# A 14-stage transformer kernel in split float32: the square sums of each stage's entry before the last step of k, weight units asked for one at a time over the first feed-forward pairs, and the keys' scaled input in a place of its own

## The reference

```python
# first block: retention layer ("ret"), then latent attention ("lat")
h = retention_layer(x, ...)                      # q, k, v, gate projections; 8 heads; group norm; w_out_a
k_nope, k_rope, v = shared_latent_kv(h, ...)     # w_kv_a, rmsnorm of the latent, w_uk, w_uv
h = mla_layer(h, ...)                            # w_in_b, w_uq, softmax attention, gate, w_out_b
# second block: short convolution ("mix") in layer 0, differential attention ("dif") in layer 1
for i in range(2):
    h = rms_norm(x, g_pre_mix[i])
    mix = short_conv_mixer(h, ...) if i == 0 else diff_attention(h, k, v, ...)
    # where i == 1: k, v = split(rms_norm(x, g_kv) @ w_kv), a gain of its own on the same x
    x = x + rms_norm(mix, g_post_mix[i])
    # "ffn0", "ffn1"
    gate, up = split(causal_dwconv(rms_norm(x, g_pre_ffn[i]) @ w_up), 2)
    x = x + rms_norm((silu(gate) * up) @ w_down, g_post_ffn[i])
    # "ple0", "ple1"
    g = sigmoid(rms_norm(x, g_pre_ple[i]) @ w_gate)
    x = x + rms_norm(g * (p[i] @ w_proj), g_post_ple[i])
```

## Time and profile before

| | |
|---|---|
| median of 3 runs | 2166.62 us |
| the profiled execution | 2169.12 us |
| its span | 2167.3 us |
| PE busy | 1997.5 us (92%) |
| DVE busy | 1220.8 us (56%) |
| ACT busy | 824.7 us (38%) |
| granted TensorE clock, mean | 0.965 of full speed |

### The profile page before, as it was taken

The page is one execution under the profiler, slowest core; times in us unless marked ns, Lnnn a source line. Parts: engine busy times, 40 slices in busy tenths (PEclk is TensorE's granted clock), DMA queues, the critical chain, the costliest instruction groups (busy, mean ns, idle before and its releaser), DMA issues.

```text
span 2167.3 us, 25399 instructions
## 1 busy us (share of the span) xinstructions
PE 1997.5 (92%) x9756; PEld 1666.3 (77%) x9756; DVE 1220.8 (56%) x1981; ACT 824.7 (38%) x1339; POOL 379.6 (18%) x300
## 2 busy tenths in 40 slices
PE   7999999988889999988999999798998889999996
PEld 6888888867678777876888787677787768887875
DVE  6565665256555454356777524566664577774245
ACT  4232323233465433333444323335454344442232
POOL 3322331111232210120111011221011211110111
PEclk9999999989999999999999999899999999999998
DMA  4222222222111233322223322231111212333311
GB/s 162 82 74 93 78 83 88 88 67 81 60 38 49 71 101 103 103 73 78 97 98 98 107 87 78 68 114 55 58 40 59 82 65 97 97 108 107 97 64 54
DMA packets 53664, 178.91 MB, mean 83 GB/s; under 512 B 6151, under 2 KB 8711, under 8 KB 53544
## 3 DMA queue, kind: packets, MB, share of 16 engines
q1 hardware_dynamic: 53544, 177.29, 24.7%
HBM read 172.55 MB, written 4.72 MB: 82 GB/s over the span
## 4 chain that ended last, share of the span: by engine, by line
PE 55%; DVE 12%; ACT 5%; issue 4%; POOL 1%; DVEq 0%; POOLq 0%; ACTq 0%
PE pb L780 51%; DVE WL L763 3%; ACT WH L754 2%; DVE X L947 1%; DVE FR L981 1%; PE pb L880 1%; ACT T L967 1%; PE pb L864 1%; PE pb L2405 0%; PE pb L1993 0%; DVE T L941 0%; DVE FD L1979 0%; PE pb L868 0%; DVE FD L1982 0%; ACT T L2543 0%
## 5 line engine op out<-in xcount | busy, mean ns | idle before, releaser
L780 PE MATMUL pb<-FR,WH 128*128 128x512 f32 x4552 | 1443.8, 399 | 93.3 <-DVE WL L763 40.8
L780 PEld LDWEIGHTS pb<-FR,WH 128*128 128x128 f32 x4552 | 861.3, 192 | 291.5 <-issue 57.2
L780 PE MATMUL pb<-FR,WL 128*128 128x512 f32 x2276 | 899.8, 395 | 0.0
L763 DVE TENSOR_TENSOR WL<-stage,WH 128x1024 fp32r<-128x1024 f32 x311 | 409.1, 1336 | 502.1 <-ACT WH L754 501.5
L780 PEld LDWEIGHTS pb<-FR,WL 128*128 128x128 f32 x2276 | 435.5, 191 | 93.8
L754 ACT ACTIVATE WH<-stage 128x1024 fp32r<-128x1024 f32 x311 | 318.2, 1051 | 116.9 <-PE pb L780 104.1
L780 PE MATMUL pb<-WH,FR 128*128 128x256 f32 x832 | 155.8, 285 | 3.8 <-DVE T L1098 1.5
L780 PE MATMUL pb<-FR 128*128 128x256 f32 (+3 forms) x752 | 124.3, 316 | 21.3 <-DVE T L1305 12.2
L780 PEld LDWEIGHTS pb<-FR 128*128 128x128 f32 x752 | 112.7, 195 | 36.0 <-DVE T L1305 14.8
L780 PEld LDWEIGHTS pb<-WH,FR 128*128 128x128 f32 x832 | 131.6, 192 | 5.1 <-DVE T L1098 1.9
L973 POOL TENSOR_TENSOR acc<-acc,T 128x512 f32<-128x512 f32 x56 | 75.3, 1344 | 276.8 <-ACT T L967 276.2
(11 more groups left out here) (221 smaller groups left out, 1646.9 us busy)
## 6 DMA issues: line engine op xcount, KB each, us to landing
stage<-in_ws SPq DMA_DIRECT2D x311, 512.0 KB, 3.5
X<-in_xT SPq DMA_DIRECT2D x8, 256.0 KB, 5.6
FD<-in_decay SPq DMA_DIRECT2D x8, 256.0 KB, 3.7
FD<-scr SPq DMA_DIRECT2D x1, 2048.0 KB, 9.6
out_dram<-X SPq DMA_DIRECT2D x8, 256.0 KB, 2.0
scr<-FD SPq DMA_DIRECT2D x10, 160.0 KB, 5.8
FD<-in_rope_b SPq DMA_DIRECT2D x2, 512.0 KB, 3.7
FD<-in_pT SPq DMA_DIRECT2D x4, 256.0 KB, 5.6
```

The lines of the kernel that those rows point to most:

```text
L763: dve.tensor_tensor(lo, src, hi.bitcast(F32), ALU.subtract).then_inc(*self.tick("w_lo", ("w_lo", u)))
L780: m = pe.matmul(out, l, r, start=first and i == 0, stop=last and i == n - 1)
```

## The change

1. `pe_entry` does the sums after step 6 of k (before the last step) and the spread after step 7. Before, both came after step 7, with five steps of the next tile between them.
2. `dve_entry` and `act_entry` take one more block (`more`) and make its unit behind the root and ahead of R.
3. In the feed-forward stages the units of pair m come from `ffn_ahead`: one or two units in turn (the tiles 2; 3; 4 and 5; 6; 7 and 8; 9; ...) until pair 11, and as before from there. Before it was tile 2 at pair 1, tile 3 at pair 2, none at pair 3, two units at every later pair. Two units of the down projection are made ahead of the last two `back`.
4. In lat, mix, ple and dif the first units after the entry are asked for earlier in the same way. In lat the calls on gate tiles 0 and 1 stay in place and the first finds its unit made.
5. In dif the keys' input of steps 0 to 3 lies in a free part of `FR`, with no wait for the queries; for steps 4 to 7 it stays in place.

```diff
-    def pe_entry(self, pe, s, cover):
+    def pe_entry(self, pe, s):
         self.pe_wide(pe, s, [(name, c, self.xin(o)) for name, c, o in WIDE[s]],
-                     [(s, "w", n) for n in range(len(WIDE[s]))], KD, lambda k: ("xg", s, k), {})
-        self.pe_sums(pe, (s, "pre"), ("acc", s, "x", 7))
-        cover({4: lambda: self.pe_spread(pe, (s, "pre"))})
+                     [(s, "w", n) for n in range(len(WIDE[s]))], KD, lambda k: ("xg", s, k),
+                     {KD - 2: lambda: self.pe_sums(pe, (s, "pre"), ("acc", s, "x", 7)),
+                      KD - 1: lambda: self.pe_spread(pe, (s, "pre"))})
...
         self.dve_rms(dve, (s, "pre"), 1024)
+        self.lo_to(dve, more)
...
+    def ffn_ahead(self, L, m):
+        t = max(2 * m - 5, m + m // 2)
+        return BLOCK[f"w_ffn_up_2_{L}", KD - 1, 3 + t // 2 + NF * (t % 2)]
...
         for m in range(NF):
-            if m in (1, 2):
-                self.lo_to(dve, BLOCK[name, KD - 1, 3 + NF * (m - 1)])
-            if m >= 3:
-                self.lo_to(dve, BLOCK[name, KD - 1, m + NF])
+            self.lo_to(dve, self.ffn_ahead(L, m))
             front(m)
+            if m == NF - 1:
+                self.lo_to(dve, BLOCK[down, 1, 3])
             if m:
                 back(m - 1)
+        self.lo_to(dve, BLOCK[down, 3, 3])
         back(NF - 1)
...
         for m in range(8):
-            if m >= 2:
-                self.lo_to(dve, BLOCK["w_sc_in_2", KD - 1, m])
+            if m:
+                self.lo_to(dve, BLOCK["w_sc_in_2", KD - 1, m if m >= 2 else 18])
...
+    def dif_xkv(self, p, k):
+        return self.fr(D0 + 18432 + 2048 * p + 512 * k, 512) if k < 4 else self.xin(0)(p, k)
...
-        for k in range(KD):
-            self.lo_to(dve, BLOCK["w_q_2", k, 7])
-            for h in {0: (0, 1, 2), 1: (3,), 2: (4,), 3: (5,)}.get(k, ()):
-                query(h)
-            dve.wait_ge(*self.at("xkv_hi", k))
-            dve.scalar_tensor_tensor(out=xin(1, k), in0=self.xt(k), scalar=self.col("g_kv_2", k),
...
-        for h in (6, 7):
+        for h in range(3):
             query(h)
+        for k in range(4):
+            key_input(k)
+        for h in range(3, 6):
+            query(h)
+        self.lo_to(dve, BLOCK["w_q_2", KD - 1, 7])
+        query(6)
+        for k in range(4, KD):
+            key_input(k)
+        query(7)
```

More of the change, by code:

```diff
@@ L1013, in act_entry @@
                 self.hi_to(act, BLOCK[WIDE[s][-1][0], k, WIDE[s][-1][1]])
+        self.hi_to(act, more)
         self.act_spread(act, (s, "pre"), self.R)
@@ L1995, in bias, with tile @@
                     *self.tick("pe_bias", ("pe", "mix", "bias", h, i)))
-        def tile(m, i, between=None):
-            self.pe_tile(pe, ("mix", "p", m, i), "w_sc_in_2", (8 + m, 16 + m, m)[i], KD, xin, None, between)
-        self.pe_entry(pe, "mix", lambda between: tile(2, 0, between))
+        def tile(m, i):
+            self.pe_tile(pe, ("mix", "p", m, i), "w_sc_in_2", (8 + m, 16 + m, m)[i], KD, xin)
+        self.pe_entry(pe, "mix")
         for m in range(2, 8):
@@ L2003, in pe_mix @@
             for i in range(3):
-                if (m, i) != (2, 0):
-                    tile(m, i)
+                tile(m, i)
                 if i < len(rows):
@@ L2123, in pe_ffn @@
     def pe_ffn(self, pe, s, L):
[L2124 to L2129, removed]
+        self.pe_entry(pe, s)
+        for m in range(3, NF):
             for i in range(2):
-                tile(m, i)
+                self.pe_tile(pe, (s, "up", m, i), f"w_ffn_up_2_{L}", m + NF * i, KD, self.xin(0))
         self.pe_out(pe, s, self.ffn_in, lambda k: ("ffn_m", s, k), {})
     def act_ffn(self, act, s, L):
-        name, M = f"w_ffn_up_2_{L}", self.ffn_m
+        down, M = OUT[s][0], self.ffn_m
         def back(m):
@@ L2169, in dve_ffn @@
     def dve_ffn(self, dve, s, L):
-        name = f"w_ffn_up_2_{L}"
+        down = OUT[s][0]
         def front(m):
@@ L2256, in pe_ple @@
         self.pe_spread(pe, (s, "post"))
-        def gate(m, between=None):
-            self.pe_tile(pe, (s, "gate", m), f"w_ple_gate_2_{L}", m, KD, self.xin(0), None, between)
-        self.pe_entry(pe, s, lambda between: gate(6, between))
-        gate(7)
+        self.pe_entry(pe, s)
+        for m in (6, 7):
+            self.pe_tile(pe, (s, "gate", m), f"w_ple_gate_2_{L}", m, KD, self.xin(0))
         for m in range(3, 8):
@@ L2386, in key @@
         def key(h):
-            self.pe_tile(pe, ("dif", "k", h), "w_kv_2", h, KD, xin, (lambda k: ("xkv", k)) if h == 0 else None,
+            self.pe_tile(pe, ("dif", "k", h), "w_kv_2", h, KD, self.dif_xkv, (lambda k: ("xkv", k)) if h == 0 else None,
                          h and {1: lambda: scores(h - 1, 1), 4: lambda: scores(h - 1, 2),
@@ L2391, in value @@
         def value(c, halves, between=None):
-            self.pe_natural(pe, "dif", c, "w_kv_2", (8 + 2 * c, 9 + 2 * c), KD, xin, None, halves, between)
+            self.pe_natural(pe, "dif", c, "w_kv_2", (8 + 2 * c, 9 + 2 * c), KD, self.dif_xkv, None, halves, between)
         def scores(h, i):
@@ L2455, in out, with query @@
             self.pe_out_steps(pe, "dif", DIF_OUT[group], self.dif_zin, lambda k: ("dif_z", k))
-        def query(m, between=None):
+        def query(m):
             for k in range(KD):
@@ L2466, in query @@
                 i.then_inc(*self.tick("pe_proj", ("unit", u), ("xq_free", k), *done))
-                if between and k in between:
-                    between[k]()
-        self.pe_entry(pe, "dif", lambda between: query(6, between))
+        self.pe_entry(pe, "dif")
+        query(6)
         query(7)
@@ L2514, in act_dif, with key_input @@
     def act_dif(self, act):
-        QZ, xin = self.dif_qz, self.xin(0)
+        QZ = self.dif_qz
+        def key_input(k):
+            if k >= 4:
+                act.wait_ge(*self.at("xq_free", k))
+            act.activation(self.dif_xkv(0, k), self.xt(k), ACT.Copy, scale=self.col("g_kv_2", k)).then_inc(
+                *self.tick("xg_hi", ("xkv_hi", k)))
         def query(h):
```

89 lines of the change are left out of this document (47 added, 42 removed).

## The result

The changed kernel takes 2116.31 us (median of 4 runs, 2113.96 to 2117.57), the kernel before, run beside it, 2168.82 (2166.03 to 2174.74). The ratio is 0.975, with a 95% interval of 0.973 to 0.978: 52.5 us less. The profiled execution took 2117.57 us for a span of 2115.8.

What follows compares the result with a forecast made beforehand. PE, busy 92%, was taken to bound the kernel. Gains of 17.3 + 17.2 + 3.2 + 5.4 + 2.5 + 0.7 + 6.0 = 52.3 us take 2166.62 to 2114; range 2106 to 2130.

Steps and rivals of the forecast that it cites:

- the two signs of being wrong: The prediction is wrong if a gap stands at tiles 12 to 17, or if lat's gain is under 3 us.
- Part 1: Stage entries: sums ahead of step 7 bring R and ffn0's first front 4.0 us earlier; PE itself gains 0.57.
- Parts 2 and 3: Both ffn: tile 4's wait goes, 12.0 us, and the down projection's, 5.3; ffn0 gains 17.3, ffn1 17.2.
- rival (b): In ffn the gap returns around tiles 13 to 16, as units pay 0.5 to 1 us beside POOL; 2120 to 2132, chance 0.15.
- Part 4, mix: Mix: tile 2's unit is made ahead of R, so its 2.57 us wait and 0.6 of the entry go: 3.2 us.
- Part 4, lat: Lat: on DVE's chain R comes 4.2 us earlier and the unit's 1.2 lies ahead of R: 5.4 us.
- Ple0: Behind ple0's last projection: fourth output 2.1 us earlier, the unit behind it saves 0.4: 2.5 us.
- ple1: In ple1 the same output already waits for PE, so only PE's 0.7 us of the entry is gained.
- Part 5: Dif: the keys' input made ahead gains 6.2 us, less 0.2 for the clock: 6.0; a 3.5 us wait stays at step 4.

Runs made afterwards that it cites:

- g2_fill_heads: The changed kernel with unread identity matmuls (6, 8, 8, 4) in PE's idle time in lat's heads 0, 1, 3 and 5; 2108.65 us, ratio 0.971.

## Why the prediction was right, and where it was wrong

**Right as a whole.** Forecast 2114 (2106 to 2130), measured 2116.31; no rival happened. All that was to be seen stood there: no L763 wait on PE behind the launch, fronts 4.3 us nearer to the entry, ffn0 at full rate in one piece, one wait at step 4 of key 0, 5.21 us behind ple0's last projection. Of the two signs of being wrong, one came: lat's gain under 3 us.

**Part 1, fronts 4 us nearer.** Ffn0's first front was set at 982.9, which is 37.9 us behind step 0 of the entry (945.01 before). It came 37.5 behind it (975.12 - 937.58).

**Parts 2 and 3, ffn.** DVE's row of units was laid out from the front. Moved to the new entry, the units of tiles 4, 6 and 7 were due at 986.8, 996.5 and 1004.8, and began at 986.46, 996.13 and 1004.66. The unit at 996.13, one of those beside POOL's rounding, took 1.47 us, 0.24 more than that of 978.16, and the pairs of units took 1.3 each. So rival (b), by which every unit would pay 0.5 to 1 us for POOL, is out. The Trainium skill's rule on the shared way to SBUF (GPSIMD Engine Reference, Specifications) states the contention and no size; the trace agrees with it at a quarter of a microsecond for such a unit. It was so little because the overlap is short: POOL's rounding ran from 995.22 to 996.51, beside the first 0.38 us of the unit. In the 2.26 us unit of the earlier trace rows POOL's adds ran beside the first 1.17 us. The down units, priced at 5.3, cost 5.7 and 6.7 when they are taken out, which leaves 12.3 and 11.5 of 18.0 and 18.2 for the first pairs with the sums, priced at 12.0. These are not sums of independent parts: the old pairs cost 9.7 and 8.7, the sums alone give 4.3, and with the down units' 5.7 that is more than 18.0, since the edits share one lead.

**Part 4, mix: too small.** Predicted 3.2, measured 5.2. I priced the wait of 2.57 us at its length and left out the clock behind it, although I had charged just that, 1.5 us, behind the two gaps of ffn. It was there in the kernel before, and isn't after:

```profile
792.00:796.00 4.00, 4.00 (x13) 0.57 0.81 271
```
```profile
792.00:796.00 4.00, 4.00 (x19) 1.00 0.00 0
```

0.43 x 4.0 is 1.7 us; 3.2 + 1.7 = 4.9.

**Part 4, lat: the step that failed.** "R comes 4.2 earlier and the unit's 1.2 us lies ahead of R: 5.4 us." The chain on DVE was right, and what it takes from PE was not looked at. The account against -5.4:

- In the entry, +1.6. Behind a wait of 1.11 us PE went to 1.2 GHz at 490, in the very steps that R waits for. The filler kernel's entry is the same code with a wait of 1.12, and didn't drop:

```profile
490.00:494.00 4.00, 4.00 (x12) 0.57 0.57 194
```
```profile
491.10:495.10 4.00, 4.00 (x23) 1.00 0.54 185
```

  There the first latent came 45.06 us behind step 0, in the changed kernel 46.67, in the kernel before 49.41. So R could come 4.35 us earlier (forecast 4.2), and came 2.74 earlier.
- From head 0's waiting transposes on, +5.6, with 10.2 us of full speed lost in place of 3.4.

-5.4 + 1.6 + 5.6 = +1.8, measured +1.5. The step that failed is that the lead of DVE's chain would last to the end of the stage: the term put the clock behind lat's waits at nothing, in the entry and in the heads. With no drop in the heads nor at 490, lat is 8.9 under before, as `g2_fill_heads` shows. I had said that I would be wrong if lat's gain was under 3 us, and there I was.

**Ple0, ple1.** Ple0 2.2 for 2.5. Ple1 came out 1.5 longer instead of 0.7 shorter. The same code took 76.8 to 79.2 us over the changed kernel and the versions with its ple1. In the kernel before the eight sums at its very end ran at full clock and the spread began 3.66 us behind them (2148.85 to 2152.51); in the changed kernel they ran at 1.2 GHz, and it is 5.21 (2095.75 to 2100.96). That is the 1.5. The 0.7 of the entry isn't seen either: up to these sums ple1 is as long as before within 0.2 us.

**Part 5, the keys' input.** Queries 0 to 2 came 38.4 us behind the entry's step 0 (due 38.2), though DVE met a new wait for a DMA there:

```profile
1418.73 0.36 DVE L2758 TENSOR_TENSOR T<-T 128x64 f32<-128x64 f32 x2 [2.07 <-DMA T<-in_lam]
```

It costs the 0.2 us by which they were late, at most. The wait at step 4 of key 0 was 3.94 us for 3.5. The gain was 7.1 for 6.0: before, three more waits stood behind the first one, with PE at 1.2 GHz from 1461 to 1472,

```profile
1462.03 1.22 PE L780 MATMUL pb<-FR,WH 128*128 128x512 f32 x2 [2.13 <-DVE FR L2757]
...
1465.18 1.22 PE L780 MATMUL pb<-FR,WH 128*128 128x512 f32 x2 [1.50 <-DVE FR L2757]
...
1468.34 1.22 PE L780 MATMUL pb<-FR,WH 128*128 128x512 f32 x2 [1.51 <-DVE FR L2757]
```

 and I took the clock off the gain (0.2). By (1 - clock) x time PE lost 5.1 us of full speed there before and loses 1.7 now, so it had to be added, though how much of it lay beside DVE's pace wasn't tried.

**The sum came out by luck in part.** Lat's 6.9 us and ple1's 2.2 were missing in the profile; ret's 3.7, which no part of the change makes, mix's 2.0, ffn's 1.7 and dif's 1.1 nearly made up for them.

## What to carry to other kernels

Price a gap with the clock behind it, wherever it stands, and ask then whether PE is the one that is waited for in that stretch: the same low clock cost 3.1 us for each head in lat and nothing at the stage borders, where DVE sets the pace. When a change moves a stretch in time, its own waits may be the same to the hundredth and its clock another; short unread matmuls in the waits removed this. And an edit that uses up a lead should be judged together with the one that makes it: the sums alone gave 20.7, the units alone 36.4, the keys alone nothing that can be measured. Where a single part is tried, compare it stage by stage: both totals hold a lat that is 5 to 6 us longer.

## What the runs showed of the hardware that I had not expected

- A wait of 2.24 to 2.29 us in lat's heads dropped the granted clock to 1.2 GHz in some heads and not in others (head 3 before: not; after: for 6.8 us). A wait of 1.83 us in head 0 did not and one of 1.85 did, and in lat's entry a wait of 1.11 us did and one of 1.12 did not. The length of the wait alone doesn't tell.
- In lat's heads one such drop showed in the records for 3.4 or 6.8 us, and cost 1.7 or 3.4 us of full speed (3.1 in time for the longer one, by the heads with fillers). Over the heads, 3.4, 5.1, 10.2 and 11.9 us of full speed lost went with 2.0, 3.5, 7.2 to 7.8 and 8.7 to 9.1 us of time.
- Matmuls of a 128x128 identity, 8 in a wait of 2.26 us, kept the clock at 2.4 GHz through all the heads, and the transposes behind them still began when ScalarE's input came (0.25 to 0.51 us of idle left ahead of them).
- Ret, the same code in all versions, took 447.6 to 452.1 us in the profiles of this case.
